# Eight of the 22 gate-and-up tiles of each feed-forward part by Strassen's seven block products

## What is computed

```python
h = rms_norm(x, gain)
f = (silu(h @ w_gate) * (h @ w_up)) @ w_down
x = x + f            # in the first block: x + rms_norm(f, gain)
```

## Time and profile before

| | |
|---|---|
| median of 3 runs | 1959.91 us (1959.9 to 1960.38) |
| the profiled execution | 1960.69 us, of which the span from first to last instruction is 1958.9 us |
| granted TensorE clock | 1.00 over the whole span |
| busy: PE, PE weight loads, DVE, ACT, POOL | 1952.4, 1601.0, 909.8, 815.5, 768.7 us |
| DMA | 177.39 MB, 91 GB/s on average |

### The profile page before, as it was taken

The page is one execution under the profiler, slowest core; times in us unless marked ns, Lnnn a source line. Parts: engine busy times, 40 slices in busy tenths (PEclk is TensorE's granted clock), DMA queues, the critical chain, the costliest instruction groups (busy, mean ns, idle before and its releaser), DMA issues.

```text
span 1958.9 us, 26026 instructions
## 1 busy us (share of the span) xinstructions
PE 1952.4 (100%) x9055; PEld 1601.0 (82%) x9055; DVE 909.8 (46%) x1184; ACT 815.5 (42%) x1098; POOL 768.7 (39%) x307
## 2 busy tenths in 40 slices
PE   9999999999999999999999999999999999999999
PEld 6777888888888888888888888888777788888887
DVE  5775654343146456454243434224788764343200
ACT  6664533232244433434332323225888752323211
POOL 4223444444424334343444444443222244444443
PEclk9999999999999999999999999999999999999999
DMA  5212122222323222222232223232111122222322
GB/s 173 73 64 90 65 97 96 96 96 103 103 73 115 80 86 91 70 96 75 93 100 96 96 96 113 89 99 85 55 64 53 55 97 96 96 96 96 110 98 93
DMA packets 49012, 177.39 MB, mean 91 GB/s; under 512 B 5568, under 2 KB 6464, under 8 KB 48960
## 3 DMA queue, kind: packets, MB, share of 16 engines
q1 hardware_dynamic: 46656, 172.95, 26.2%
q10 hardware_dynamic: 2304, 3.74, 0.6%
HBM read 174.57 MB, written 2.10 MB: 90 GB/s over the span
## 4 chain that ended last, share of the span: by engine, by line
PE 98%; DVE 1%; ACT 0%; DMA 0%; issue 0%; SPq 0%; DVEq 0%; ACTq 0%
PE B L363 26%; PE B L364 26%; PE B L372 26%; PE B L1277 2%; PE B L1085 1%; PE B L1089 1%; PE B L1086 1%; PE B L384 1%; PE B L389 1%; PE B L385 1%; PE B L1266 1%; PE B L1322 1%; PE B L913 1%; PE B L944 1%; PE B L929 1%; PE B L1131 1%
## 5 line engine op out<-in xcount | busy, mean ns | idle before, releaser
L608 POOL TENSOR_TENSOR WL<-RAW,WH 128x1024 fp32r<-128x1024 f32 (+1 forms) x296 | 757.7, 2562 | 1162.5 <-PE B L372 753.1
L363 PE MATMUL B<-HH,WH 128*128 128x512 f32 x1608 | 628.2, 391 | 0.3 <-DVE QT L2195 0.3
L364 PE MATMUL B<-HL,WH 128*128 128x512 f32 x1608 | 626.1, 389 | 0.0
L344 ACT CAST WH<-RAW 128x1024 fp32r<-128x1024 f32 (+1 forms) x300 | 329.1, 1098 | 521.4 <-PE B L364 444.6
L372 PE MATMUL B<-HH,WL 128*128 128x512 f32 x1608 | 398.3, 390 | 0.0
L363 PEld LDWEIGHTS B<-HH,WH 128*128 128x128 f32 x1608 | 301.8, 188 | 64.8 <-issue 1.7
L372 PEld LDWEIGHTS B<-HH,WL 128*128 128x128 f32 x1608 | 301.4, 188 | 63.2 <-POOL WL L608 0.5
L364 PEld LDWEIGHTS B<-HL,WH 128*128 128x128 f32 x1608 | 301.9, 188 | 62.3
L1963 DVE TENSOR_TENSOR U<-B,RB 128x512 f32<-128x512 f32 x66 | 45.6, 691 | 294.3 <-PE B L372 294.3
L363 PE MATMUL B<-MH,WH 128*128 128x512 f32 x440 | 171.2, 389 | 0.0
L364 PE MATMUL B<-ML,WH 128*128 128x512 f32 x440 | 171.2, 389 | 0.0
(11 more groups left out here) (392 smaller groups left out, 2376.9 us busy)
## 6 DMA issues: line engine op xcount, KB each, us to landing
RAW<-in_w_small SPq DMA_DIRECT2D x254, 512.0 KB, 3.2
RAW<-in_w_large SPq DMA_DIRECT2D x48, 704.0 KB, 4.0
out_t<-X SPq DMA_DIRECT2D x7, 256.0 KB, 4.4
X<-in_x_t ACTq DMA_DIRECT2D x4, 256.0 KB, 6.8
X<-in_x_t SPq DMA_DIRECT2D x4, 256.0 KB, 7.1
DECAY<-in_decay ACTq DMA_DIRECT2D x4, 256.0 KB, 2.6
RAW<-in_w_small ACTq DMA_DIRECT2D x2, 256.0 KB, 7.1
RAW<-in_w_small SPq DMA_DIRECT2D x2, 256.0 KB, 7.9
```

The costliest lines, as they stand in the source:

```text
L344: act.copy(wh, raw).then_inc(s_hi, 1)
L363: pe.matmul(bank, wh[:, c, :], xh[:, k0 + c, :], start=(start and c == 0), stop=False)
L364: mm = pe.matmul(bank, wh[:, c, :], xl[:, k0 + c, :], start=False, stop=False)
L608: pool.tensor_tensor(wl, raw, wh.bitcast(F32), ALU.subtract).then_inc(s_lo, 1)
```

## The change

The first 8 hidden tiles of each part (`NS = 8`) are no longer pairs. The gate and up weights of such a tile together are 256 outputs by 1024 inputs; cut in half both ways (A11, A12 gate, A21, A22 up) and with the input cut in halves by features and by positions, Strassen's scheme (in Winograd's form) gives gate and up from seven products of half size: each 4 chunks x 3 matmuls of 128x128 by 256 columns, 84 matmuls of 256 columns where the pair had 48 of 512. The other 14 tiles (`NC = 14`) remain pairs.

A part now begins with 4 pairs (`PRO`), then come 8 rounds `seven(i)`, each one Strassen tile woven with one pair, then 2 pairs. What comes new to each engine:

- **TensorE**: the products, in banks B[4], B[5], B[6] (`a`, `b`, `c_`), each after waits for its weights (`t_lo`) and for the bank to be read (`t_bank`, `t_kept`).
- **ScalarE**: it issues the loads of the Strassen weights (two of 512 KB a round, from `w_seven`), casts their high parts (`SH7`, 4096 elements per partition a round in six casts), and copies the bank `a` once (`CW`).
- **VectorE**: the weight sums (four of 128x512), the low parts (`SL7`, one of 128x1024 and five of 128x512), and seven operations of 128x256 or 128x512 on the results. GpSimd gets nothing new; its low splits go from 44 to 28 a part.
- **Input sums**, once per part: VectorE makes three sums of input blocks and a difference (`input_sums`), ScalarE casts them (`TH`), VectorE makes their low parts (`TL`), all between the opening pairs.
- **Late split**: `HD` keeps all 22 hidden tiles (it lies where `ML` is, and `SH7`, `SL7`, `TH` where `MH` is), and the casts to `MH` and the subtractions to `ML` come only in the last two pairs.

```diff
 # TensorE
+                def seven(i):
+                    gate, up = Unit(u0 + 2 * PRO, i, 2), Unit(u0 + 2 * PRO + 1, i, 2)
+
+                    pe.wait_ge(t_lo, i * 6 + (lo0 + 1))
+                    pe.wait_ge(t_bank, i * 4 + (bank0 + 3))
+                    product(Q1, HH, HL, upper, FIRST, a, start=True)
+                    product(Q2, HH, HL, lower, FIRST, b, start=True)
...
+                    product(Q7, TH, TL, T3, every, c_, start=True)
+                    pe.wait_ge(s_gate, i + (NC * f + PRO))
+                    high_part(pe, gate, B[0][:], DC, HH, HL)
...
+                    product(Q6, TH, TL, T2, every, a)
+                    low_part(pe, gate, B[0][:], DC, HH)
...
+                    pe.wait_ge(t_kept, i + (NS * f + 1))
+                    product(Q5, TH, TL, T1, every, a)
+                    pe.wait_ge(s_up, i + (NC * f + PRO))
+                    high_part(pe, up, B[1][:], DC, HH, HL)
+
+                    pe.wait_ge(t_lo, i * 6 + (lo0 + 5))
+                    pe.wait_ge(t_bank, i * 4 + (bank0 + 6))
+                    product(Q3, HH, HL, lower, SECOND, a)
+                    pe.wait_ge(t_lo, i * 6 + (lo0 + 6))
+                    product(Q4, TH, TL, T4, every, c_)
+                    low_part(pe, up, B[1][:], DC, HH)
 # ScalarE
+                def seven(i, produce=True):
+                    ahead = i + 1
+                    if produce:
+                        products_done(i, 2)
+                        act.wait_ge(t_lo, i * 6 + 6 * (group0 + 1))
+                        load(i + (group0 + 1))
+                    split_hi(act, Unit(u0 + 2 * PRO + 2, i, 2), DC)
+                    if produce:
+                        singles_hi(ahead)
+                    products_done(i, 4)
+                    act.copy(CW, B[4][:, FIRST]).then_inc(t_kept, 1)
...
+                pair(0, DC, splits[0])
+                input_block()
+                pair(1, DC, splits[1])
+                load(group0)
+                input_sums_hi()
+                pair(2, DC, splits[2])
 # VectorE
+                def seven(i, produce=True):
...
+                    if produce:
+                        products_done(i, 3)
+                        dve.wait_ge(t_lo, i * 6 + 6 * (group0 + 1))
+                        sum_7(ahead)
+                        products_done(i, 4)
+                        sum_6(ahead)
+                        sum_3(ahead)
+                        low_singles(ahead)
+                        lo(ahead, 2, Q7, s7)
+                    gate_scaled(i + PRO, B[0][:])
+                    products_done(i, 5)
+                    dve.wait_ge(t_kept, i + (group0 + 1))
+                    dve.tensor_copy(US[:, SECOND], c_).then_inc(t_up, 1)
+                    dve.wait_ge(t_up, i + (group0 + 1))
+                    dve.tensor_tensor(US[:, SECOND], US[:, SECOND], a, ALU.subtract).then_inc(t_bank, 1)
...
+                    up_and_hidden(i + PRO, B[1][:])
+                    if produce:
+                        lo(ahead, 5, Q3, S3[:])
+                        lo(ahead, 6, Q4, A22)
...
+                opening_pair(0)
+                input_sums()
+                opening_pair(1)
+                input_sums_lo()
+                opening_pair(2)
+                sum_7(0)
...
+                lo(0, 6, Q4, A22)
+                opening_pair(3)
+                dve.sem_inc(t_bank, 4)
+                with dve.Fori(0, NS - 1) as i:
+                    seven(i)
+                seven(NS - 1, produce=False)
+                gate_scaled(NC - 2, B[0][:])
+                some_hidden(range(0, 5))
+                up_and_hidden(NC - 2, B[1][:])
+                some_hidden(range(5, 14))
+                gate_scaled(NC - 1, B[0][:])
```

More of the change, by code:

```diff
@@ L800, in ffn, with product @@
                     pair(0, before)
-                with pe.Fori(4 if before is None else 1, FC) as i:
+                    for n in range(1, PRO):
+                        pair(n)
+                def product(form, xh, xl, rows, cols, bank, start=False):
+                    for c in range(4):
+                        wh, wl = SH7[:, form.start + c, :], SL7[:, form.start + c, :]
+                        pe.matmul(bank, wh, xh[:, rows.start + c, cols], start=(start and c == 0), stop=False,
+                                  skip_group_check=True)
+                        pe.matmul(bank, wh, xl[:, rows.start + c, cols], start=False, stop=False,
+                                  skip_group_check=True)
+                        mm = pe.matmul(bank, wl, xh[:, rows.start + c, cols], start=False, stop=(c == 3),
+                                       skip_group_check=True)
+                    mm.then_inc(t_product, 1)
@@ L1434, in ffn, with silu, pair @@
             def ffn(f, u0, chunks_after, ahead=()):
-                def pair(i, chunks, splits=None):
+                g_ffn = (G_FFN1, G_FFN2, G_FFN3)[f]
+                group0 = NS * f
+                def silu(i):
+                    act.wait_ge(s_gate, i + (NC * f + 1))
+                    act.activation(SG[:], G1[:], ACT.Silu).then_inc(s_silu, 1)
+                def pair(i, chunks, splits=None, between=None):
                     first, second = (Unit(u0 + 2, i, 2), Unit(u0 + 3, i, 2)) if splits is None else splits
@@ L1438, in pair @@
                         split_hi(act, first, chunks)
[L1439 to L1440 removed]
+                    silu(i)
+                    if between is not None:
+                        between()
                     if second is not None:
                         split_hi(act, second, chunks)
[L1443 to L1444 removed]
@@ L1445, in ffn, with input_block @@
-                act.preload_act_table(ACT.Silu)
[L1447 to L1451, removed]
+                def input_block():
+                    for c in range(4):
+                        act.activation(TB22[:, c, :], X[:, 4 + c, SECOND], ACT.Copy,
+                                       scale=gain(g_ffn, 4 + c)).then_inc(t_b22, 1)
@@ new lines, in hidden_hi, with some_hidden @@
+                def hidden_hi(t):
+                    if t < NS:
+                        act.wait_ge(t_hidden, group0 + t + 1)
+                    else:
+                        act.wait_ge(s_hidden, NC * f + t - NS + 1)
+                    act.copy(MH[:, t, :], HD[:, t, :]).then_inc(s_m_hi, 1)
+                def some_hidden(tiles):
+                    for t in tiles:
+                        hidden_hi(t)
+                act.preload_act_table(ACT.Silu)
+                splits = list(ahead) + [None] * (PRO - len(ahead))
@@ new lines, in ffn @@
+                pair(0, DC, splits[0])
[4 more added lines that the diff above has]
+                pair(2, DC, splits[2])
+                for hi in (singles_hi, sum_7_hi, sum_6_hi, sum_5_hi, sum_3_hi, single_4_hi):
+                    hi(0)
+                pair(3, DC, splits[3])
+                with act.Fori(0, NS - 1) as i:
+                    seven(i)
+                seven(NS - 1, produce=False)
+                products_done(NS - 1, 7)
```

244 lines of the change are left out of this document (221 added, 23 removed).

## The result

Four runs of the changed kernel took 2019.17 us in the median (2017.06 to 2023.12), those of the kernel before beside them 1960.06 (1959.9 to 1960.38). The ratio is 1.0303, 95% interval 1.029 to 1.0316: slower by 3.0%. The profiled execution took 2017.78 us, 57.1 more than that of before.

The account below looks back on a forecast made before the run. TensorE, with 98% of the chain, was taken as the bound, so any wait is lost in full. From 1960.7: -19 + 22 + 15 + 16 + 8.5 = +42.5, less 0.8, gives 2002 us; range 1988 to 2020 (80%: 1974 to 2030).

Parts of the forecast that it names:

- the five waits: TensorE's predicted holes: Q3 each round, first Q1 of each part, opening units and pairs, down projections; 0.6 to 8 us.
- Products, -19.0: TensorE, 24 Strassen tiles: 84 matmuls at 0.120 us replace 48 at 0.2265, saving 0.79 us a tile, 19.0 us.
- Loop, +22: In the rounds, Q3 waits for VectorE's late difference: 1.15 us in six of eight rounds, 7.4 a part, 22 us.
- the landing: In each round, the second of two 512 KB weight loads lands 4.9 us after the first issue; bounds 4.2 and 5.5.
- Openings of parts 2 and 3, +15: Before the rounds, late HD, G and low splits delay pair 2, pair 3 and first Q1: 7.4 us each, 15 us.
- Opening of part 1, +16: Units 6 and 7 wait for casts (4.1, 4.3 us), first Q1 for banks (7.9): 16 us, bounds 9 and 20.
- Ends, +8.5: Each part's down projection waits 2.5 us for the last G, its second unit 0.3: 2.8 a part, 8.5 us.
- The clock, rival 4: TensorE's clock halves after seven waits over 4 us, 5.4 us each, +38: 2040 us; chance 0.03.
- Rival 1: GpSimd's turns don't fall into VectorE's chains; no loop or end waits, smaller opening waits: 1957 us; chance 0.12.
- Rival 2: The loop's wait ahead of Q3 is hidden, the other costs stay: +20.5, 1980 us; chance 0.13.
- Rival 3: More is late: loads land at 5.5 us and over, register instructions between VectorE's waits show: 2027 us and above; chance 0.10.

Follow-up runs that it names:

- the short splits: Changed kernel with GpSimd subtracting only one of eight chunks per unit in the first and third part, to time queues only: 1978.2 us, ratio 1.0095.
- the first experiment: Changed kernel with VectorE's copy and difference for product Q3 moved ahead of two low splits and the gate scaling: 1998.92 us, ratio 1.0187.

## Why the prediction was right, and where it was off

The direction and the mechanism held: 2002 us forecast, 2019 measured, with the five waits at the places and behind the instructions that the prediction named. That the median lies inside the range of 1988 to 2020, by 0.8 us, is luck in part: two of the four executions lie above it, and a cost of 12.9 us that the sum left out was met by openings and ends put 9.5 us too high. By its steps:

- **Products, -19.0.** Measured -17.3. 0.120 us per matmul is right; the seams between 256 and 512 columns (1.84 and 3.65 us for parts of 1.81 and 3.62) were not in the sum and leave 0.72 us a tile instead of 0.79.
- **Loop, +22.** The mechanism is as told; the size was 32.2. The first round cost 0.50 (a wait of 0.23 and 0.27 around it), near the 0.55, the last nothing, but the six between 1.6 to 2.0 (waits of 1.34 to 1.72) and not 1.15. This is the term of the sum that was mis-sized most, and the step in it is the landing: the first sum began 5.3 to 5.7 us after the first issue, not 4.9. By the prediction's own slope (0.6 us of landing for 0.65 of wait) that gives 1.6 to 2.0 a round, which is what came. The row of a pair that it took was two loads of SP 0.48 us apart; those of ScalarE landed 0.3 us and more later.
- **Openings of parts 2 and 3, +15.** Measured 11.8: 5.1 and 6.6.
- **Opening of part 1, +16.** Measured 11.2: waits of 3.80 and 2.44 for the casts (4.1 and 4.3 forecast) and 4.18 for the banks (7.9). The turn of GpSimd that stood aside for the low splits in this profile and held them in others is 3 us of it.
- **Ends, +8.5.** Measured 7.0.
- **The clock, rival 4.** Given 0.03, at 5.4 us behind each of seven waits over 4 us (the prediction's own terms name five such waits, so 27 us by its price and not 38). This is the step that failed, a term put at nothing in the sum: half clock followed seven waits, six of them shorter than 4 us, for 1.5 to 2.7 us each, 12.9 in all. It isn't the whole of a rival but a price on waits of about 2 us and more (seven of eight here), which belonged in the sum. Without it this profiled execution would be at 2004.9 us, where the sum for it was 2003.2.
- **Rival 1** (turns don't collide) is excluded by the trace, where the turns lie in the chains, and the short splits show what it would have been worth: in the two parts that have them no waits ahead of Q3 and the down projections, and openings that cost 12.1 us in the first part, half clock included, and 2.2 in the third (12 and 1.9 in the prediction). **Rival 2** (the loop's wait is hidden) didn't come. **Rival 3** came in part: the landing at 5.3 to 5.7 us, around its 5.5. (Its terms of 12 and 15 us on 2002 add up to 2029, not 2027.)

Of the 14.6 us between the sum for a profiled execution (2003.2) and this one (2017.8) 12.9 are the clock, 10.2 the loop, 1.7 the seams, and the openings and ends gave back 9.5; 0.7 are outside. That register instructions between waits cost anything was not tried by itself.

## What to carry to other kernels

A change that saves a tile 0.7 us of TensorE and adds twelve dependent steps on other engines is decided by their order: the order written cost 57 us, another one, with a tile less in each part, gave 10. Look for the closed chain of a loop (which release leads back to itself) and put what releases a load first; a wait that is removed may only uncover the next, so read the trace after each move. Price a wait of TensorE of about 2 us and more with what may follow it at half clock, here 1.5 to 2.7 us.

## What the runs showed of the hardware

- TensorE's clock fell to half after waits of 1.88 to 7.26 us, not after each of them, and never after waits up to 1.77 us. At half clock (granted 0.50) the step from one matmul to the next was 0.213 us for 256 columns and 0.427 for 512; behind a wait such matmuls ran for 6.0 us at most.
- Nine matmuls of no use in a wait of the third part kept the clock at 1.00, where it had been 0.50.
- When a split of GpSimd began 0.05 to 0.06 us ahead of the next of VectorE's operations, it held that operation (2.83 to 2.89 us instead of 0.69) or stood aside for two (3.55 to 3.61 us instead of 2.4), one or the other at the same place of the same instructions. The first Q1 came 3.0 us later or earlier by this in the first part and 1.4 in the others. The Trainium skill, SBUF — State Buffer, section "Who interferes with whom", says that the one that issues first has the port for its whole instruction; the second pair of rows in the first experiment agrees, while in the first GpSimd began 0.05 us earlier and still stood aside.
